# One output store per block of 32 tokens in place of four, in a one-core hybrid attention and PEER step

## The chip, the cores and the metric

The kernel runs on one core of a Trainium2 chip. The metric is the device time in microseconds (us) of one execution; the figure given for a kernel is the median of several runs.

## The reference, cut to what matters

One layer of a streaming encoder is computed for 512 prompt tokens and 32 sample tokens of width 1024: two attention mixers merged by gates, and then PEER, a retrieval over 16384 experts. For each token PEER picks 16 experts in each of 8 heads, 128 in all, takes a dot product with each expert's row of `u`, and sums the experts' rows of `v` with the weights that come of it. The change lies where the last sum leaves the chip:

```python
x = x + out
x = x + _peer(_rms(x, ln2_g), peer_wq, peer_subkeys, peer_u, peer_v)
# in _peer, for a block of tokens t and its chosen experts e with weights g:
a = jax.nn.gelu(jnp.einsum('td,thkd->thk', t, u[e]))
return jnp.einsum('thk,thkd->td', (g * a.astype(jnp.float32)).astype(t.dtype), v[e])
# y_prompt = x of the prompt without its 16 meta tokens, y_sample = x of the sample
```

## The kernel before, in words

Tokens stand in five tiles: the sample tile of 32 tokens comes first, then four prompt tiles of 128. The work behind the attention is cut into **17 blocks** of 32 tokens (`BLOCKS`): one for the sample, four for each prompt tile. A block has 32 **columns** (`SG`). A column is one gather: GpSimd's queue (POOL) fetches 128 rows of `peer_uv`, one for each of 32 tokens times 4 groups, each row 8 KB (an expert's `u` and `v` side by side), 1 MB in all, into one of nine buffers `rows` (`RING`). Partition 32a + t of a column belongs to token t and group a.

For each column:

- VectorE (DVE) takes the dot product of the `u` half with the token's row in `ps_h` (`dot`, L2580), and after every second column prepares the argument of the gelu (`arguments`, L2587 to L2590).
- ScalarE (ACT) makes of that a weight and a 128 x 32 matrix `diag` (`diagonals`, L2117 to L2126).
- TensorE (PE) multiplies `diag` with the `v` half and adds to `ps_v` in PSUM (`mix`, L1793): 16 matmuls, in four groups of 256 output columns. Group a's 32 partitions of `ps_v` hold columns 256a to 256a + 255 of the block's 32 tokens.
- The gather of column c waits until the mix of column c - 9 is done (`s_pv`), since it reuses that buffer.

When a block's 32 columns are mixed, ACT copies `ps_v` into `yo`, one of two buffers of 128 x 256 (`block_out`, L2134), and issues the stores on its own DMA queue. PE begins the next block with the residual (`residual`, L1784) once the copy is done. ACT's program is fixed: it calls `block_out(n)` and right after it `diagonals` for the first two columns of the next block. `block_out` waits for `s_out` of the same `yo` buffer, so for the stores of two blocks earlier. The last wait of the program, on the SyncE queue (SP), is for all stores (L1293).

Beside all that, while blocks are mixed, the attention of the next tile runs in slices between the columns (`front`, spread over a tile's 128 columns by `ticks_at`); its weights come as 512 KB loads on SP's queue into four buffers `wch`. Behind the last tile's attention (about 1421 us) only columns are left. So three queues feed the core's 16 DMA engines: POOL's with the gathers, SP's with the weights, ACT's with the stores.

The stores before, in `block_out`:

```python
t = tile(i)
for a in range(GROUPS):
    dst = io.y_prompt[P * t + GROUP * g:P * t + GROUP * (g + 1), :] if t < 4 else io.y_sample[:, :]
    act.dma_start(dst[:, QD * a:QD * (a + 1)], yo[GROUP * a:GROUP * (a + 1), n % 2, :]).then_inc(s_out[n % 2], 16)
```

Here `GROUPS` is 4, `GROUP` 32 and `QD` 256: each store takes 32 partitions, 1 KB from each, to 32 rows of the output that lie 4 KB apart.

Of the kernel before, what the change touches and what calls it, by code (L numbers as in the profile page):

```python
# [28 lines left out]
P = 128  # L29
# [658 lines left out]
GROUP = 32  # L688
GROUPS = P // GROUP
# [3 lines left out]
NB = len(BLOCKS)  # L693
# [6 lines left out]
QD = D // GROUPS  # L700
# [19 lines left out]
def first_block(i):  # L720

    return BLOCKS.index((i, 0))
# [182 lines left out]
def stream(nc, io, m, sem):  # L905
# [22 lines left out]
    tan, weight, diag, yo, rows = m.tan, m.weight, m.diag, m.yo, m.rows  # L928
# [53 lines left out]
    def tile(i):  # L982
        return ORDER[i]
# [92 lines left out]
    def slot_of(p, j):  # L1076
        return place[(p, j)] % WRING
# [5 lines left out]
    def uses_of(p, j):  # L1083

        n = place[(p, j)]
        return len(loads[n % WRING:n + 1:WRING])
# [22 lines left out]
    with psum("ps_h", [P, D]) as ps_h, psum("ps_v", [P, QD]) as ps_v, \  # L1109
# [102 lines left out]
        s_out = [sem(f"s_out{i}") for i in range(2)]  # L1212

        @block.sync
        def _(sp):
            def load(p, j, src, n=D):
                if place[(p, j)] >= WRING:
                    p0, j0 = loads[place[(p, j)] - WRING]
                    sp.wait_ge(s_wu[slot_of(p0, j0)], uses_of(p0, j0))
                sp.dma_start(wch[slot_of(p, j)][:, 0:n], src).then_inc(s_wl[slot_of(p, j)], 16)  # L1220

            def load_gate(p, n):
                j, a = divmod(n, 2)
                load(p, G_AT + n, io.w_gate[DC * a + j, :, :, :].rearrange("p c k -> p (c k)"))

            def load_x(i):
                t = tile(i)
                if i >= 2:
                    sp.wait_ge(s_xc, first_block(i - 1))
                if t < 4:  # L1230
                    sp.dma_start(xb[i % 2][:, :], io.x_prompt[P * t:P * (t + 1), :]).then_inc(s_x[i % 2], 16)
                else:
                    sp.dma_start(xb[i % 2][0:DEC, :], io.x_sample[:, :]).then_inc(s_x[i % 2], 16)

            for p, members in enumerate(PASSES):
                if p:
                    i, = members
                    t = tile(i)
                    sp.wait_ge(s_av, 2 * H * (i - 1))
                    if p == 1:  # L1240
                        sp.wait_ge(s_tile_out.sem, s_tile_out.upto(DC))
                        sp.wait_ge(s_used, 1)
                    sp.dma_start(tab, io.tabs[:, t, :]).then_inc(s_tab, 16)
                    for n in range(WRING):
                        load(p, J_AT + n, io.w_row[n, :, :])
                    load_x(i)
                    for n in range(WRING, 12):
                        load(p, J_AT + n, io.w_row[n, :, :])
                    rest = DC * (COLS - 3 * 512)
                    load(p, J_AT + 12, io.w_row[12, :, 0:rest], rest)  # L1250
                    for k in range(2):
                        load(p, U_AT + k, io.w_uq[:, k, :], H * AQK)
                    load(p, V_AT, io.w_ukv[:, :])
                    for n in range(WRING):
                        load_gate(p, n)
                    sp.wait_ge(s_norm, p)
                    for dst, c0, w in OUT_COLS:
                        sp.dma_start(io.new_p[dst][META + P * t:META + P * (t + 1), :], pr[:, c0:c0 + w]).then_inc(s_new, 16)
                else:
                    for n in range(2 * SOON, 2 * SOON + WRING):  # L1260
                        load_gate(p, n)
                    for i in members:
                        load_x(i)
                    sp.dma_start(spare, io.keyb[:, :].rearrange("(a p) k -> p a k", a=GROUPS)).then_inc(s_spare, 16)
                for n in range(WRING + (0 if p else 2 * SOON), 2 * DC):
                    load_gate(p, n)
                if p:
                    for j in range(DC):
                        load(p, Z_AT + j, io.w_o[j, :, :])
                    for k in range(DC):  # L1270
                        load(p, O_AT + k, io.w_out[k, :, :])
                    for n in range(PH):
                        load(p, Q_AT + n, io.peer_wq[ASKED[n], :, :, :].rearrange("p c k -> p (c k)"))
                    continue
                sp.wait_ge(s_fav, 4)
                for k in range(DC // 2):
                    sp.dma_start(out_w[k], io.w_out[k, :, :]).then_inc(s_out_a.sem, 16)
                for j in range(WRING):
                    load(p, Z_AT + j, io.w_o[j, :, :])
                sp.wait_ge(s_ave, 2)  # L1280
                for k in range(DC // 2, DC):
                    sp.dma_start(out_w[k], io.w_out[k, :, :]).then_inc(s_out_b.sem, 16)
                for j in range(WRING, DC):
                    load(p, Z_AT + j, io.w_o[j, :, :])
                sp.wait_ge(s_fo, 1)
                sp.wait_ge(s_ot, 2)
                for c in ASK_REST:
                    sp.dma_start(ask_w[c], io.ask_rows[c, :, :]).then_inc(s_ask_w.sem, 16)
                sp.dma_start(key0, io.keyb[:, :]).then_inc(s_key0, 16)
                for c in ASK_RING:  # L1290
                    load(p, Q_AT + c, io.ask_rows[c, :, :])
            for a in range(2):
                sp.wait_ge(s_out[a], 16 * GROUPS * ((NB + 1 - a) // 2))  # L1293
            sp.wait_ge(s_new, 16 * 5 * (NP - 1))

        @block.gpsimd
# [24 lines left out]
        def _(pe):  # L1321
# [105 lines left out]
            def turn(i, u):  # L1427
                a = tile_unit(i, u)
                q = queries(i)
                pe.wait_ge(s_prob, a + 1)  # L1430
                if a:
                    pe.wait_ge(s_ptc, a)
                if u % H == 0 and earlies(i, u):
                    pe.wait_ge(s_pmc, earlies(i, u))
                for j, (c, r, _) in enumerate(chunks(i)):
                    ins = nc.tensor.transpose(turned()[0:r, j, 0:q], prob[a % 2][0:q, c:c + r], ident[0:q, 0:q])
                ins.then_inc(s_pt, 1)
# [57 lines left out]
            def few_turn(n):  # L1495
                pe.wait_ge(s_fprob, n + 1)
                if n:
                    pe.wait_ge(s_fptc, n)
                else:
                    pe.wait_ge(s_fcopy, 1)  # L1500
                for j, (c, r, _) in enumerate(few_chunks):
                    ins = nc.tensor.transpose(few_turned()[0:r, j, :], few_prob[n % 2][:, c:c + r], ident[:, :])
                ins.then_inc(s_fpt, 1)
# [310 lines left out]
        def _(act):  # L1814
# [314 lines left out]
            def block_out(n):  # L2129
                i, g = BLOCKS[n]  # L2130
                act.wait_ge(s_pv, SG * (n + 1))
                if n >= 2:
                    act.wait_ge(s_out[n % 2], 16 * GROUPS * (n // 2))
                nc.scalar.copy(yo[:, n % 2, :], ps_v[:, :]).then_inc(s_yo, 1)  # L2134
                act.wait_ge(s_yo, n + 1)
                t = tile(i)
                for a in range(GROUPS):
                    dst = io.y_prompt[P * t + GROUP * g:P * t + GROUP * (g + 1), :] if t < 4 else io.y_sample[:, :]
                    act.dma_start(dst[:, QD * a:QD * (a + 1)], yo[GROUP * a:GROUP * (a + 1), n % 2, :]).then_inc(s_out[n % 2], 16)

            for _ in front(0):
                pass
            for b in range(NCOL + LAG):
                if b % SLOTS == 0 and b // SLOTS + 1 < NP:
                    ahead = front(b // SLOTS + 1)
                if b >= SG and b % SG == LAG - 1:
                    block_out(b // SG - 1)
                if 2 <= b <= NCOL and b % 2 == 0:
                    diagonals(b - 2)
                if b < NCOL:  # L2150
                    n = b // SG
                    for _ in range(ticks_at(b)):
                        next(ahead)
                    if n + 1 < NB and b % SG == 17:
                        softmax(n + 1)
# [600 lines left out]
```

## Time and profile before

| what | value |
|---|---|
| median of 3 runs | 1814.53 us (1811.41 to 1815.37) |
| the profiled execution's own time | 1823.78 us |
| its span in the profile | 1822.0 us |
| DVE, PE, ACT, POOL busy, share of the span | 72%, 69%, 32%, 29% |
| moved by DMA | 696.47 MB, mean 382 GB/s |
| of it the gathers on POOL's queue | 570.53 MB |
| chain that ended last | DMA 36%, PE 27%, DVE 23% |

The span is the profiled execution without its start and end outside the trace. Busy shares are means over the whole span. The page cuts the span into 40 slices of 45.6 us and gives for each the busy tenths of every engine and the mean share in which the 16 DMA engines were busy. The stages are: up to 336 us the weights' first part and the first attention tiles; 336 to 1421 us columns with attention between them; 1421 to 1818 us columns alone; then the last store.

### The profile page before, as it was taken

To read this page: it belongs to the slowest core of one execution; us is meant where nothing else is said; L and a number is where in the kernel's file an instruction comes from. 1 tells how busy PE (TensorE), PEld (TensorE's weight loads), DVE (VectorE), ACT (ScalarE), POOL (GpSimd) and SP (SyncE) were. 2 spreads that over 40 slices of the span, in tenths; PEclk is the share of its full clock that TensorE was granted. 3 is DMA by queue.
4 is the path that set the end of the run, shared out by engine and by line. 5 is a ranking of instruction groups with operands and counts; after the bars stand their busy time and mean duration, and the time that the engine had idled before them with its cause. 6 is when DMAs were issued, how large, how long until landed. Compare 5 with 4: busy or idle time off the path is not lost.

```text
span 1822.0 us, 26376 instructions
## 1 busy us (share of the span) xinstructions
PE 1255.3 (69%) x9056; PEld 701.2 (38%) x9056; DVE 1308.2 (72%) x3842; ACT 581.8 (32%) x1997; POOL 524.0 (29%) x569
## 2 busy tenths in 40 slices
PE   8999776778877576778887576778877443434343
PEld 4668442444544233444544233445535111111111
DVE  5662676898766577798766676998676768686754
ACT  2332133433323333333422333343423322222222
POOL 0100123333323322332332222332322433333332
PEclk9989889787888687877898697887999555555555
DMA  6237399999999999899999999999999999999997
GB/s 263 72 100 279 157 394 423 401 425 424 426 424 423 422 416 422 351 407 405 422 422 422 424 422 390 408 389 386 424 422 424 424 427 426 426 427 424 427 421 301
DMA packets 119380, 696.47 MB, mean 382 GB/s; under 512 B 17983, under 2 KB 21118, under 8 KB 49102
## 3 DMA queue, kind: packets, MB, share of 16 engines
q0 software_dynamic: 78848, 570.53, 75.1%
q1 hardware_dynamic: 36686, 121.83, 17.3%
q10 hardware_dynamic: 3712, 2.43, 0.4%
q8 instruction: 72, 1.18, 0.2%
q14 instruction: 62, 0.51, 0.1%
HBM read 691.65 MB, written 3.02 MB: 381 GB/s over the span
## 4 chain that ended last, share of the span: by engine, by line
DMA 36%; PE 27%; DVE 23%; issue 5%; ACT 4%; POOL 1%; ACTq 0%; DVEq 0%; POOLq 0%
DMA rows<-in_peer_uv,index 26%; DVE rows L2580 9%; PE ps_v L1793 6%; PE ps_f L1546 4%; DMA wch<-in_w_row 4%; PE ps_f L1561 2%; DMA wch<-in_w_out 2%; PE ps_h L1773 2%; PE ps_f L1340 2%; DMA wch<-in_w_uq 1%; PE ps_f L1424 1%; PE ps_f L1464 1%; PE ps_f L1640 1%; DVE score L2289 1%; DMA wch<-in_peer_wq 1%
## 5 line engine op out<-in xcount | busy, mean ns | idle before, releaser
L2580 DVE CUSTOM_DVE_ANT_0 rows<-rows,ps_h 128x1024 f32<-128x1024 f32 x544 | 656.6, 1220 | 286.1 <-DMA rows<-in_peer_uv,index 235.5
L1317 POOL DMA_INDIRECT rows<-in_peer_uv,index x544 | 514.1, 945 | 1197.7 <-PE ps_v L1793 1007.9
L1793 PE MATMUL ps_v<-rows,diag 128*32 128x256 f32 x4352 | 424.7, 508 | 425.0 <-ACT diag L2126 425.0
L1793 PEld LDWEIGHTS ps_v<-rows,diag 128*32 128x32 f32 x4352 | 126.1, 131 | 677.8 <-ACT diag L2126 568.4
L2117 ACT ACTIVATE tan<-arg 128x2 f32<-128x2 f32 x272 | 55.5, 204 | 787.8 <-DVE arg L2590 764.0
L2120 ACT ACTIVATE weight<-tan,lead 128x1 f32<-128x1 f32 x544 | 180.8, 379 | 9.1
L2126 ACT ACTIVATE diag<-sel,weight 128x32 f32<-128x32 f32 x544 | 140.7, 305 | 0.1
L1546 PEld LDWEIGHTS ps_f<-bufh,wch 128*128 128x128 f32 x768 | 114.1, 233 | 21.2 <-issue 19.0
L1546 PE MATMUL ps_f<-bufh,wch 128*128 128x128 f32 x768 | 120.3, 322 | 0.0
L1340 PE MATMUL ps_f<-wch,bufh 128*128 128x512 f32 (+1 forms) x192 | 81.7, 565 | 27.8 <-DMA wch<-in_w_row 26.8
L1569 PE MATMUL ps_f<-wch,bufb 128*128 128x512 f32 x96 | 49.8, 650 | 19.7 <-DMA wch<-in_w_out 17.6
L1340 PEld LDWEIGHTS ps_f<-wch,bufh 128*128 128x128 f32 x192 | 32.8, 202 | 71.3 <-issue 34.9
L1640 PE MATMUL ps_f<-bufh,wch 128*128 128x128 f32 x384 | 53.8, 298 | 6.4 <-DMA wch<-in_peer_wq 6.3
L1640 PEld LDWEIGHTS ps_f<-bufh,wch 128*128 128x128 f32 x384 | 49.1, 207 | 18.9 <-issue 9.8
L1561 PE MATMUL ps_f<-bufq,wch 128*128 128x128 f32 x384 | 54.3, 300 | 1.3 <-ACT bufq L1957 1.2
L1561 PEld LDWEIGHTS ps_f<-bufq,wch 128*128 128x128 f32 x384 | 49.5, 209 | 13.0 <-issue 10.4
L1773 PE MATMUL ps_h<-hrows,rep 32*128 32x512 f32 x68 | 49.3, 861 | 2.8 <-DVE dots L2580 2.8
L2589 DVE TENSOR_TENSOR lead<-dots,halfw 128x2 f32<-128x2 f32 x272 | 43.9, 161 | 9.4
L2580 DVE DVE_READ_ACCUMULATOR2_ANT dots<- 128x1 f32 x544 | 44.9, 82 | 0.0
L1424 PE MATMUL ps_f<-bik,bufb 64*128 64x144 f32 (+2 forms) x96 | 38.9, 492 | 7.5 <-ACT kt L1878 6.7
L2587 DVE SCALAR_TENSOR_TENSOR cube<-dots 128x2 f32<-128x2 f32 x272 | 42.8, 158 | 0.6
L2590 DVE SCALAR_TENSOR_TENSOR arg<-cube,dots 128x2 f32<-128x2 f32 x272 | 42.2, 155 | 0.0
(389 smaller groups left out, 1690.0 us busy)
## 6 DMA issues: line engine op xcount, KB each, us to landing
wch<-in_w_gate SPq DMA_DIRECT2D x60, 512.0 KB, 8.1
wch<-in_w_row SPq DMA_DIRECT2D x36, 512.0 KB, 12.3
wch<-in_w_o SPq DMA_DIRECT2D x32, 512.0 KB, 7.7
wch<-in_w_out SPq DMA_DIRECT2D x24, 512.0 KB, 11.2
wch<-in_peer_wq SPq DMA_DIRECT2D x24, 512.0 KB, 12.6
rows<-in_peer_uv,index POOLq DMA_INDIRECT x544, 13.6
w_tok<-in_w_tok SPq DMA_DIRECT2D x4, 1640.0 KB, 13.6
wch<-in_w_uq SPq DMA_DIRECT2D x6, 384.0 KB, 12.3
```

What stands on the lines that cost most here:

```text
L1317: pool.indirect_dma_start(rows[c % RING][:, :, :].rearrange("p a d -> p (a d)"), None, io.peer_uv[:, :], at).then_inc(s_uv[c % RING], 16)
L1340: ins = nc.tensor.matmul(ps_f[:, 2 + c % 2, 0:cols], buf_h[:, k, :], w[:, b, :], start=(k == 0), stop=(k == DC - 1))
L1424: ins = nc.tensor.matmul(ps_f[0:q, u % 2, 0:nk], left, right, start=True, stop=True)
L1546: ins = nc.tensor.matmul(gated(p)[:, a, :], w[:, k, :], h_of(p)[:, k, 0:n], start=(k == 0), stop=(k == DC - 1))
L1561: ins = nc.tensor.matmul(blended(p, j)[:, x, :], w[:, x, k, :], ot_of(p)[:, x, k, 0:n], start=(k == 0), stop=(k == 3))
L1640: ins = nc.tensor.matmul(ps_f[:, 2 + n % 2, 0:x], w[:, k, :], h_of(p)[:, k, 0:x], start=(k == 0), stop=(k == DC - 1))
L1773: ins = nc.tensor.matmul(ps_h[:, 512 * j:512 * (j + 1)], rep[here, :, :].rearrange("p a m -> p (a m)"), hrows[i % 2][here, 512 * j:512 * ( ...
L1793: ins = nc.tensor.matmul(ps_v[GROUP * a:GROUP * (a + 1), :], diag[:, c % DRING, :], rows[c % RING][:, 1, QD * a:QD * (a + 1)], start=False ...
L2117: nc.scalar.activation(tan[:, s:s + 2], arg[:, s:s + 2], ACT.Tanh, scale=TANH).then_inc(s_tan, 1)
L2120: nc.scalar.activation(weight[:, s + j:s + j + 1], tan[:, s + j:s + j + 1], ACT.Identity, scale=lead[:, s + j:s + j + 1], bias=lead[:, s + ...
L2126: nc.scalar.activation(diag[:, (c + j) % DRING, :], sel[:, :], ACT.Copy, scale=weight[:, s + j:s + j + 1]).then_inc(s_diag, 1)
L2580: v.tensor_tensor_reduce(out=u, in0=u, in1=ps_h[:, :], scale=1.0, scalar=0.0, op0=ALU.mult, op1=ALU.add, accum_out=dots[:, c % KEEP:c % KE ...
```

## The change

The four stores of a block become one. Its source is all 128 partitions of `yo`; its target is the same region of the output, written as group, token, column: 4 x 32 x 256. It counts 16 instead of 64 on `s_out`, and the two waits on `s_out` are adapted. Nothing else differs.

```diff
@@ -1290,7 +1290,7 @@
             for a in range(2):
-                sp.wait_ge(s_out[a], 16 * GROUPS * ((NB + 1 - a) // 2))
+                sp.wait_ge(s_out[a], 16 * ((NB + 1 - a) // 2))
             sp.wait_ge(s_new, 16 * 5 * (NP - 1))
@@ -2130,13 +2130,12 @@
                 if n >= 2:
-                    act.wait_ge(s_out[n % 2], 16 * GROUPS * (n // 2))
+                    act.wait_ge(s_out[n % 2], 16 * (n // 2))
                 nc.scalar.copy(yo[:, n % 2, :], ps_v[:, :]).then_inc(s_yo, 1)
                 act.wait_ge(s_yo, n + 1)
                 t = tile(i)
-                for a in range(GROUPS):
-                    dst = io.y_prompt[P * t + GROUP * g:P * t + GROUP * (g + 1), :] if t < 4 else io.y_sample[:, :]
-                    act.dma_start(dst[:, QD * a:QD * (a + 1)], yo[GROUP * a:GROUP * (a + 1), n % 2, :]).then_inc(s_out[n % 2], 16)
+                dst = io.y_prompt[P * t + GROUP * g:P * t + GROUP * (g + 1), :] if t < 4 else io.y_sample[:, :]
+                act.dma_start(dst.rearrange("t (a c) -> a t c", a=GROUPS), yo[:, n % 2, :]).then_inc(s_out[n % 2], 16)
```

On ACT, at the end of each of the 17 blocks, between the copy of the block's sum and the first weights of the next block, the program reads (- before, + now; a DMA row gives the target's shape):

```order
 L2126 ACTIVATE diag<-sel,weight 128x32 x2
 L2134 COPY yo<-ps_v 128x256
-L2139 DMA out_y_prompt<-yo 32x256 x4
+L2138 DMA out_y_prompt<-yo 4x32x256
 L2117 ACTIVATE tan<-arg 128x2
 L2120 ACTIVATE weight<-tan,lead 128x1 x2
```

Four issues have become one in the same place, the target's outermost size is now 4 where each store had 32 before, and no other instruction has moved.

## Rows read from the trace of the kernel before

**Rows 1.** The page's slices: DMA's busy tenths and GB/s, 40 slices of the span

```profile
DMA  6237399999999999899999999999999999999997
GB/s 263 72 100 279 157 394 423 401 425 424 426 424 423 422 416 422 351 407 405 422 422 422 424 422 390 408 389 386 424 422 424 424 427 426 426 427 424 427 421 301
```

**Rows 2.** Windows from block end to block end (columns in the first line), core 0

```profile
core 0: us, PE busy (x) PEld busy (x) DVE busy (x) ACT busy (x) POOL busy (x), PEclk, DMA share, GB/s
336.00:426.00 90.00, 71.74 (x506) 44.83 (x502) 81.08 (x250) 32.09 (x120) 31.63 (x33) 0.79 1.01 416
...
730.00:826.00 96.00, 72.00 (x503) 43.33 (x505) 79.82 (x231) 34.10 (x120) 29.46 (x32) 0.79 0.94 382
826.00:919.00 93.00, 78.72 (x568) 47.51 (x569) 74.00 (x218) 34.98 (x132) 30.63 (x33) 0.83 1.00 414
...
1025.00:1134.00 109.00, 68.12 (x400) 30.96 (x401) 80.14 (x235) 39.01 (x115) 31.22 (x34) 0.80 0.99 410
1134.00:1227.00 93.00, 72.96 (x546) 48.71 (x544) 87.34 (x241) 33.50 (x115) 30.21 (x32) 0.85 0.99 398
1227.00:1322.00 95.00, 81.13 (x604) 52.63 (x596) 75.57 (x217) 37.38 (x132) 29.95 (x32) 0.86 0.98 405
...
1502.00:1582.00 80.00, 34.95 (x272) 10.85 (x276) 59.49 (x178) 21.17 (x83) 30.24 (x33) 0.53 1.01 426
...
1742.00:1818.00 76.00, 31.38 (x264) 9.68 (x264) 41.85 (x108) 20.66 (x80) 22.77 (x25) 0.52 0.88 369
```

**Rows 3.** The chain that ended last, in order of time (start, us, what), 1592 to 1652 us

```profile
1592.24 14.30 DMA rows<-in_peer_uv,index
1611.96 15.16 DMA rows<-in_peer_uv,index
1632.54 14.10 DMA rows<-in_peer_uv,index
```

**Rows 4.** DMA view of 1581 to 1592 us, one block's four stores in it

```profile
DMA packets 812, 4.64 MB, mean 422 GB/s; under 512 B 135, under 2 KB 263, under 8 KB 263
q0 software_dynamic: 618, 4.48, 96.8%
q10 hardware_dynamic: 192, 0.13, 3.7%
```

**Rows 5.** The instructions of the store's line and their landing

```profile
L2139 ACTq DMA_DIRECT2D out_y_prompt<-yo x64: 321/442/1249, 426.9 to 1820.0; - x64
DMA to landing us min/median/max: 5.0/6.3/8.3
```

**Rows 6.** Timeline at a block's end, 729 to 733 us, and at the program's end

```profile
729.95 1.74 ACTq L2139 DMA_DIRECT2D out_y_prompt<-yo  x4
731.73 0.20 ACT L2117 ACTIVATE tan<-arg 128x2 f32<-128x2 f32 x1 [1.82 <-issue]
...
1818.30 0.37 ACT L2134 COPY yo<-ps_v 128x256 f32<-128x256 f32 x1 [1.84 <-PE ps_v L1793]
1818.70 1.74 ACTq L2139 DMA_DIRECT2D out_y_prompt<-yo  x4
```

**Rows 7.** Issues of other transfers: two loads on ACT's queue, one three-dimensional load on SP's

```profile
L303 ACTq DMA_DIRECT2D bik_c<-in_bk_t x1: 560/560/560, 0.7 to 0.7; - x1
L304 ACTq DMA_DIRECT2D bik_c<-in_ik_t x1: 611/611/611, 1.3 to 1.3; - x1
L1264 SPq DMA_DIRECT2D kt<-in_keyb x1: 482/482/482, 83.3 to 83.3; - x1
```

**Rows 8.** DMA view of 1816 to 1822 us, nothing but the last block's stores in it

```profile
DMA packets 192, 0.13 MB, mean 22 GB/s; under 512 B 64, under 2 KB 192, under 8 KB 192
q10 hardware_dynamic: 192, 0.13, 7.9%
```

**Rows 9.** The page's queues (q1 SP's, q10 ACT's): packets, MB, share of 16 engines

```profile
q1 hardware_dynamic: 36686, 121.83, 17.3%
q10 hardware_dynamic: 3712, 2.43, 0.4%
```

**Rows 10.** Window of 732 to 742 us, columns as in Rows 2

```profile
732.00:742.00 10.00, 6.89 (x32) 2.93 (x33) 4.44 (x14) 5.15 (x15) 1.88 (x2) 0.50 0.52 186
```

## The prediction, made before the changed kernel ran

> **What bounds the kernel now.** I began with the slices of the page [rows 1]: from the sixth slice to the last but one the DMA engines show 9 tenths or more in all but one, at up to 427 GB/s, whatever PE and DVE do. Then I asked for windows cut at the block ends [rows 2]. There are 16 of them from 336 to 1818 us. In 11 the DMA share is 1.00 to 1.02; four are below, 0.94, 0.99, 0.99 and 0.98; the last shows 0.88, only because its final 11 us have no gathers left, and I count it with the 11 as full: 12. The chain of waits says the same from the other side: behind 1421 us it is one gather after another, each 14 to 15 us in flight, and from one to the next about 20 us, in which 8 columns go by [rows 3]. So a column costs 80/32 = 2.5 us [rows 2], the time in which 16 engines move 1 MB. A gather spends its 14 us in line behind five others; nothing that an engine of the core does faster there is worth anything. What counts is **how long each of the 16 DMA engines works**, and since a gather is complete only when all of its 128 rows have landed, the busiest of the 16 sets the pace.
>
> The four stores of a block are small in this: 192 packets, 3.7% of 16 engines over 11 us, which is 6.5 us of engine time, or 0.4 us on each engine if all take the same share [rows 4]. That all do is shown by the count. 192 is 4 times 48, and 48 is the 32 rows of a store and 16 completions, one from each engine; where the last four stores are alone, 64 of the 192 are under 512 B and 128 are of 1 KB [rows 8]. Each engine writes two rows of every store.
>
> **The change, part by part.**
>
> *The issues on ACT.* Four issues take 1.74 us, and the next block's first weights stand behind them [rows 6]. One issue of the new form is not in the trace. From below it is bounded by 0.32, the shortest of the stores now [rows 5]; from above by 0.61, an issue on ACT's queue early in the program; a three-dimensional load on SP's queue took 0.48 [rows 7]. I take 0.6, as those two are ACT's own and nothing else shows ACT issuing anything but 32 rows in the steady part. So ACT gets 1.74 - 0.6 = 1.1 us back at each block end (1.4 at most). Who waited for it: tan, weight, diag, then the mix, then the gather that reuses the buffer. In a stretch with the DMA engines full that gather would only stand in line earlier: nothing. At 729.95 it is different. The engines are half idle just behind it (0.52 over 732 to 742 us [rows 10]), and ACT's 1.74 us lie on the way there. I count 1.1 us of gain once. At 1134 and 1227 the stretches are below 1.00 too, but the chain there runs through PE and DVE rather than ACT's issues, so nothing.
>
> *The rows among the DMA engines.* Now the source's outermost size is 128 and the target's is 4. The trace has no transfer whose two sides differ in that, so the price is bounded from both sides. If the 128 rows are still dealt to 16 engines, each has 8 rows and one completion, as now: 0. If the deal follows the target's outermost size, four engines carry all 128 rows, 32 each, and the other twelve none. I take the second. The nearest row is SP's packet count [rows 9]: by the code its 264 transfers have 32463 rows, and with 16 completions each that would be 36687 packets; there are 36686. One completion is missing, and one transfer, the load of `brow`, has 15 rows: it ran on 15 engines. So the number of engines comes from the size of a dimension, and is not always 16; here a size of 4 allows four.
>
> This is also what the Trainium skill says (DMA: Bandwidth & Descriptors, section Why a DMA increments its semaphore by 16 and not by 1): the number of engines is the largest up to 16 that divides the slowest dimension of both sides, which would be 4 here. The trace agrees with it for 15 rows and 32 rows, and shows nothing for 4 against 128. By that rule the sum is the one that follows; without it, the first rival's.
>
> The price: a block's data now costs 6.5 us of engine time [rows 4]. Were all of it the 128 rows, a row costs 0.051 us; were completions as dear as rows, 0.034. Four engines do 24 rows more than before, so 24 x 0.034 to 24 x 0.051 = **0.8 to 1.2 us more on each of the four**, for each block. I take 1.1, near the upper end because the 64 small packets carry almost nothing. The other twelve get 0.4 us less, which helps nobody.
>
> *How often that counts.* 16 stores are followed by gathers. Where the engines are full (12 stretches), the four engines fall behind by 1.1 us, the gathers complete 1.1 us later, and so does everything behind: 12 x 1.1 = 13.2 us. In the four stretches below 1.00 something else leads; 0.06 x 96 = 5.8 us idle in the first and 1 to 2 us in the others hide 1.1 us each: 0. The cover there is that idle time.
>
> *The wait for the old store.* A store lands after 5.0 to 8.3 us [rows 5]. With 33 packets on an engine, taken in turn with gather rows of 0.31 us (96.8% of 176 us over 547 rows, the 618 packets less the 71 completions [rows 4]), it will take 33 x (0.31 + 0.05) = 12 us and about one more to start. `yo` is needed again two blocks, 160 us, later: free.
>
> *The end.* Now the last issue ends at 1820.4 and the span at 1822.0 [rows 6, 8]. With one issue the work starts about 1.1 us sooner, but four engines need 32 x 0.05 = 1.6 us for it instead of some 0.2 for the last 32 rows: 0, within 0.3.
>
> **Sum:** -1.1 + 13.2 + 0 = **+12.1 us**. The profiled execution takes 1823.8 us, 9.3 above the median of the runs; its sum would be 1835.9, and on the median it makes 1814.5 + 12.1 = 1826.6 us. Its own range: at the least the five stores behind 1421 us, where only gathers are left, and five of the others at 0.8, less 3 for ACT: +5. At the most 16 at 1.2: +19. So 1819.5 to 1833.5.
>
> **The rivals.**
>
> *Sixteen engines share the new store (faster).* It decides if the deal follows the 128 rows of the source. For it: both sides have 128 rows of 1 KB in the same order, and every 128-row transfer of SP's is on 16 engines by the packet count. Against: the 15-row load, and a target that has to be walked by group first. Then the DMA work is as before less 48 completions, ACT's 1.1 us count at 730, and the end comes 1.1 us sooner: 1814.5 - 2.2 = 1812.3. If ACT's issues also count at the two other block ends where the chain of waits passes through them (1322 and 1502, both with full engines, so I doubt it), 1810.1. The same page of the Trainium skill has a rule that speaks for this change (section Bandwidth: transfers under 64 KB are dominated by their descriptors, so batch them). The trace doesn't bear it out as a gain in time here: the rows of 1 KB stay what they are, and all four stores cost 0.4 us an engine [rows 4]. By that rule the time would be this rival's.
>
> *Four engines, but the ring hides it.* Nine buffers, six gathers in flight: a lag of 1.1 us on a queue of 14 us might be made good. For it: in 336 to 1421 us the chain is half PE and DVE. Against: a full engine cannot make good anything, and the share is 1.01. Something like a third of the forecast less ACT's part would be left: +2.5, 1817.
>
> *Four engines, and the attention pays too.* SP's weight loads run over the same four engines; where PE waits for them, the lag adds to stretches that I called free, and a 1 KB write could cost an engine more when it comes 32 times in a row. 16 x 1.2 = +19, 1833.7, or a little more.
>
> **How the numbers follow.** Forecast 0.66; sixteen engines 0.14; hidden by the ring 0.11; the attention pays too 0.09. What a measurement can tell from no change is about 0.2%, 3.6 us. Slower by more than that: 0.66 + 0.09 + 0.01 of the ring's case = 0.76. Faster: a third of the first rival, 0.05. The same: 0.19. The predicted time is the forecast's, 1826.6. The range takes in the forecast's own and the ring's case and leaves out the first rival and the tail above: 1815 to 1834.
>
> **What the changed profile would show.** ACT's queue has 3712 packets now, of which 17 x 192 = 3264 are stores. On four engines it would have 448 + 17 x 132 = 2692, on sixteen 448 + 17 x 144 = 2896: this settles the first rival alone. The store would land after about 13 us on four engines, under 5 on sixteen. Its issue should be one of 0.3 to 0.6 us. The stretches behind 1421 us should be 81 us each instead of 80, with the mean DMA share a little lower, as twelve engines run out of work now and then. I am wrong if stretches with full engines keep their length although 2692 packets are counted (then the ring hides it), or if they grow by 2 us or more (then a row costs more than 0.05 us).

## The result and the profile after

| | before | after |
|---|---|---|
| median of 6 runs each | 1814.95 us (1811.41 to 1817.31) | 1824.97 us (1821.5 to 1828.6) |
| profiled execution | 1823.78 us, span 1822.0 | 1826.15 us, span 1824.3 |

The ratio is 1.0050 with a 95% interval of 1.0031 to 1.0070: slower by 9 us, 6 to 13. The medians differ by 10.0. The forecast was +12.1 us, with a range of +0.5 to +19.5. The two profiled executions differ by only 2.4 us, since each is a single run. The part before the columns took 2.8 us less in the one of after. So from here on I compare lengths within a trace, from block end to block end.

The page of the changed kernel: its DMA lines of the slices, and its queues (packets, MB, share of 16 engines).

```profile
DMA  6227499999999999999999999999999999999996
GB/s 263 77 95 289 170 401 423 399 425 424 425 424 422 411 394 421 378 411 408 424 422 422 423 420 377 425 378 418 422 422 424 426 421 416 421 418 411 420 417 284
...
q0 software_dynamic: 78848, 570.53, 75.4%
q1 hardware_dynamic: 36686, 121.83, 17.1%
q10 hardware_dynamic: 2692, 2.43, 0.4%
```

The bytes are those of before, but ACT's queue has **2692 packets** in place of 3712 [rows 9]. The text above named two numbers: 2896 for sixteen engines, 2692 for four. It is four to the packet: 448 + 17 x (128 + 4). And behind the attention (the seven slices ahead of the last) GB/s is 411 to 421 where it was 421 to 427 [rows 1].

The last block's store alone, DMA view of 1818 to 1826 us of the changed kernel: 132 packets, 4 of them completions, against 192 and 64 [rows 8].

```profile
DMA packets 132, 0.13 MB, mean 16 GB/s; under 512 B 4, under 2 KB 132, under 8 KB 132
q10 hardware_dynamic: 132, 0.13, 5.4%
```

Stretches behind the attention in the changed kernel, cut at its own block ends (us, busy times, TensorE's clock, DMA share, GB/s). Before, the three that answer to them took 79.7, 80.5 and 79.7 us by the same copies, at 426 GB/s in the one shown [rows 2].

```profile
1499.50:1580.30 80.80, 34.56 (x268) 10.71 (x268) 59.51 (x177) 21.18 (x83) 30.00 (x33) 0.52 1.01 418
1580.30:1661.90 81.60, 35.68 (x268) 10.91 (x268) 60.64 (x178) 21.21 (x83) 30.02 (x33) 0.50 1.01 416
1661.90:1742.50 80.60, 35.67 (x268) 10.89 (x268) 59.42 (x177) 21.09 (x83) 29.89 (x33) 0.50 1.01 417
```

The engines of the core do the same work as before. The stretch is longer by about 1 us, and the DMA engines move 2% fewer bytes per us at the same recorded share. What has changed is the time recorded for a packet. The gathers' line in the DMA view of 1510 to 1730 us, of the kernel before and of the changed one:

```profile
q0 software_dynamic: 12814, 93.30, 100.6%
...
q0 software_dynamic: 12532, 91.25, 100.1%
```

By share and count, the mean packet of a gather is recorded with 0.276 us before (100.6% of 16 x 220 us over 12814) and 0.281 after. No view tells one engine from another.

The store on ACT, timeline of the changed kernel at three block ends, at 730 us, 1743 us and the last; and under it the issues among the instructions of the tile `yo`, shortest, median and longest in ns:

```profile
730.81 0.55 ACTq L2138 DMA_DIRECT2D out_y_prompt<-yo  x1
731.41 0.20 ACT L2117 ACTIVATE tan<-arg 128x2 f32<-128x2 f32 x1 [0.63 <-ACT yo L2134]
...
1742.78 0.55 ACTq L2138 DMA_DIRECT2D out_y_prompt<-yo  x1
1744.45 0.20 ACT L2117 ACTIVATE tan<-arg 128x2 f32<-128x2 f32 x1 [1.70 <-DVE arg L2589]
...
1820.16 0.37 ACT L2134 COPY yo<-ps_v 128x256 f32<-128x256 f32 x1 [1.84 <-PE ps_v L1793]
```

```profile
L2138 ACTq DMA_DIRECT2D out_y_prompt<-yo x16: 550/552/582, 423.9 to 1820.6; - x16
```

One issue takes 0.55 us in place of 1.74 for four [rows 6]. So ACT does get 1.2 us back at each block end. At 1743 it spends them waiting: the next weights start 1.7 us behind the copy because DVE's argument isn't there yet. That is the gain of the change going where it is worth nothing. At 730 the weights do start earlier.

How long the store is under way is seen in two windows of 4 us of the changed kernel, 1592 to 1596 and 1596 to 1600; the store was issued at 1580.7.

```profile
q0 software_dynamic: 227, 1.69, 99.8%
q10 hardware_dynamic: 36, 0.03, 2.4%
...
q0 software_dynamic: 236, 1.70, 101.3%
```

Its last packets fall between 11 and 15 us after the issue, where four stores landed after 6.3 [rows 5].

### The profile page after: what moved, and what is told of

Same layout as the page of the kernel before. It is cut to its first block, busy times and chain, and to the rows that moved or that the text cites. A ratio compares the mean times of both kernels' runs of the same rounds, so it can differ in the third digit from the quotient of the medians.

```text
span 1824.3 us, 26325 instructions
## 1 busy us (share of the span) xinstructions
PE 1243.4 (68%) x9056; PEld 694.1 (38%) x9056; DVE 1308.0 (72%) x3842; ACT 581.4 (32%) x1997; POOL 523.6 (29%) x569
## 3 DMA queue, kind: packets, MB, share of 16 engines
q10 hardware_dynamic: 2692, 2.43, 0.4%
## 4 chain that ended last, share of the span: by engine, by line
DMA 40%; PE 24%; DVE 22%; issue 6%; ACT 3%; POOL 1%; ACTq 0%; DVEq 0%; SPq 0%; POOLq 0%
DMA rows<-in_peer_uv,index 31%; DVE rows L2579 9%; PE ps_v L1793 5%; DMA wch<-in_w_row 4%; PE ps_f L1546 4%; PE ps_f L1561 2%; DMA wch<-in_w_uq 2%; DMA wch<-in_w_out 2%; PE ps_f L1340 2%; PE ps_h L1773 2%; DVE score L2288 1%; PE ps_f L1424 1%; POOL rows L1317 1%; DVE best L2287 1%; PE ps_f L1464 1%
## 5 line engine op out<-in xcount | busy, mean ns | idle before, releaser
L1340 PE MATMUL ps_f<-wch,bufh 128*128 128x512 f32 (+1 forms) x192 | 80.3, 556 | 28.9 <-DMA wch<-in_w_row 28.0
```

What stands on the lines that cost most here:

```text
L1340: ins = nc.tensor.matmul(ps_f[:, 2 + c % 2, 0:cols], buf_h[:, k, :], w[:, b, :], start=(k == 0), stop=(k == DC - 1))
```

## Experiments

Theory: a store whose target has 4 as its outermost size runs on four of the 16 engines; they get 24 rows more than before, 1.1 us a block, and where the engines are full the program is late by just that. The rivals: the single long transfer itself is the cost; the lag hits the attention's weights; a slow landing costs in any case; and, on the other side, ACT's issues are worth time. The kernels named "deal" and "flat" leave out the order of the output: they store the same bytes, in another order.

In the table, "behind" is the time from the end of block 12 to that of block 17 in the profiled execution, five stores, no attention; it is the difference of two starts of the `yo` copy. "Last four" is the same from the end of block 13 on, and "more per store" is a quarter of its difference to the kernel before. "Whole" is the ratio to the kernel before, run beside it, with its 95% interval.

| kernel | packets of ACT's queue | engines | behind, us | last four, us | more per store | whole |
|---|---|---|---|---|---|---|
| before | 3712 | 16 | 397.6 | 316.7 | | 1 |
| after | 2692 | 4 | 401.5 | 320.8 | 1.0 | 1.0050 (1.0031 to 1.0070) |
| deal16 | 3712 | 16 | 398.0 | 316.6 | 0.0 | 1.0015 (0.9999 to 1.0032) |
| deal8 | 3168 | 8 | 397.9 | 318.0 | 0.3 | 1.0019 (1.0000 to 1.0037) |
| deal4 | 2896 | 4 | 403.3 | 321.5 | 1.2 | 1.0070 (1.0047 to 1.0093) |
| deal2 | 2760 | 2 | 410.3 | 326.8 | 2.5 | 1.0159 (1.0133 to 1.0186) |
| flat | 2896 | 16 | 397.4 | 316.6 | 0.0 | 0.9987 (0.9971 to 1.0002) |
| late | 3352 | 4, from block 12 | 403.8 | 321.2 | 1.1 | 1.0027 (1.0011 to 1.0044) |
| early | 3052 | 4, up to block 11 | 396.3 | 316.6 | 0.0 | 1.0018 (1.0005 to 1.0030) |
| behind | 3712 | 16 | 398.1 | 316.6 | 0.0 | 0.9996 (0.9984 to 1.0008) |

The two columns are not equally sharp. Five of the kernels load the engines behind the attention alike (before, deal16, flat, early, behind). In "behind" they lie between 396.3 and 398.1 us, in "last four" between 316.55 and 316.66. The spread sits in the first stretch after the attention, which takes 79.7 to 81.4 us in these five. So a price per store is read from the last four.

### The number of engines, with four issues throughout

The edit to the kernel before, with l = 16, 8, 4, 2:

```diff
-                    act.dma_start(dst[:, QD * a:QD * (a + 1)], yo[...]).then_inc(...)
+                    act.dma_start(dst[:, QD * a:QD * (a + 1)].rearrange("(h l) c -> l h c", l=4), yo[...]).then_inc(...)
```

> Four stores a block as before, but each target is written with 16 as its outermost size (the 32 tokens of a store land in another order within the store; the rest is computed as before). Theory (the target's outermost size sets how many DMA engines carry a store, and the time comes from the load of the busiest): 16 engines, 4 x 48 = 192 packets a block, 3712 on ACT's queue; no change but for slower issues, 4 x 0.55 = 2.2 us in place of 1.74, which count once: 0 to +1 us on 1815. Stretches behind the attention 79.7 to 80.5 us as before. Rival (any target in three dimensions costs the DMA engines more): slower by 8 us or more, like the single store.

> The same with 8 as the outermost size (tokens of a store in another order). Theory: 8 engines, 4 x (32 + 8) = 160 packets a block, 448 + 17 x 160 = 3168 on ACT's queue. 16 rows on each busy engine in place of 8: 8 x 0.046 less 4 completions already there, +0.37 us a block; 12 blocks with full engines give +4.4 us. Rival (four issues cannot cost what one store cost): 0.

> The same with 4 as the outermost size (tokens of a store in another order): four issues a block, as before the change, but the load of the four engines is the changed kernel's. Theory: 4 x (32 + 4) = 144 packets a block, 2896 on ACT's queue; 24 rows more on each of four engines, +1.1 us in each of the last full stretches (80.8 us), +12 in all, and ACT's longer issues add 0 to 1: 1827. Rival (the single long transfer, or its one issue, is what costs, and not the four engines): within 3 us of before.

> The same with 2 as the outermost size (tokens of a store in another order). Theory: two engines with 64 rows each, 56 more than before: 56 x 0.046 = +2.6 us a block, stretches of 82.5 us behind the attention, 12 x 2.6 = +31 us, up to +38 if the idle time of the other four stretches no longer hides it: 1846 to 1853. 4 x (32 + 2) = 136 packets a block, 2760 on ACT's queue. Rival (the ring of nine buffers hides a lag): less than twice what deal4 shows.

The packet counts came out as expected in all four: each store has l completions. So the number of engines is the target's outermost size here, while the source's is 32 throughout. The `yo` copies on which the two columns rest, ends of blocks 12, 13 and 17 in the timeline of deal4, then of deal2:

```profile
1422.72 0.37 ACT L2134 COPY yo<-ps_v 128x256 f32<-128x256 f32 x1 [3.82 <-PE ps_v L1793]
...
1504.51 0.37 ACT L2134 COPY yo<-ps_v 128x256 f32<-128x256 f32 x1 [4.81 <-PE ps_v L1793]
...
1826.00 0.37 ACT L2134 COPY yo<-ps_v 128x256 f32<-128x256 f32 x1 [1.74 <-PE ps_v L1793]
```

```profile
1428.03 0.37 ACT L2134 COPY yo<-ps_v 128x256 f32<-128x256 f32 x1 [2.67 <-PE ps_v L1793]
...
1511.60 0.37 ACT L2134 COPY yo<-ps_v 128x256 f32<-128x256 f32 x1 [4.85 <-PE ps_v L1793]
...
1838.35 0.37 ACT L2134 COPY yo<-ps_v 128x256 f32<-128x256 f32 x1 [1.84 <-PE ps_v L1793]
```

The ends of blocks 13 and 17 in deal16, then in deal8; under them the end of block 13 before and after the change (those of block 17 are at 1818.30 and 1820.16):

```profile
1491.09 0.37 ACT L2134 COPY yo<-ps_v 128x256 f32<-128x256 f32 x1 [4.83 <-PE ps_v L1793]
...
1807.71 0.37 ACT L2134 COPY yo<-ps_v 128x256 f32<-128x256 f32 x1 [1.84 <-PE ps_v L1793]
```

```profile
1501.61 0.37 ACT L2134 COPY yo<-ps_v 128x256 f32<-128x256 f32 x1 [4.83 <-PE ps_v L1793]
...
1819.59 0.37 ACT L2134 COPY yo<-ps_v 128x256 f32<-128x256 f32 x1 [1.84 <-PE ps_v L1793]
```

```profile
1501.64 0.37 ACT L2134 COPY yo<-ps_v 128x256 f32<-128x256 f32 x1 [4.81 <-PE ps_v L1793]
...
1499.39 0.37 ACT L2134 COPY yo<-ps_v 128x256 f32<-128x256 f32 x1 [4.83 <-PE ps_v L1793]
```

And a window of deal2 between two of its block ends:

```profile
1593.50:1675.50 82.00, 35.31 (x268) 10.88 (x268) 60.01 (x178) 21.16 (x82) 29.96 (x33) 0.52 1.00 412
```

Against deal16, over the last four stores, one with 8 rows more on the busiest engines (deal8) costs (317.98 - 316.62)/4 = 0.34 us, with 24 more (deal4) (321.49 - 316.62)/4 = 1.22, with 56 more (deal2) (326.75 - 316.62)/4 = 2.53: 0.043, 0.051 and 0.045 us a row. The price is near to proportional to the load of the busiest engine, and it is paid on eight engines too. The whole time says the same, less sharply: +12.7 us (8.5 to 16.9) for deal4, where 12 was expected, and +28.9 (24 to 34) for deal2, a little short of the 31 to 38 expected. deal4 has four issues as before the change and is as slow as the change or slower, so the single long transfer is not the cost. The ring's rival wanted deal2 at less than twice deal4; it is at 2.1 times in the last four stores and 2.3 times in the whole.

deal8 should have cost 0.37 us a store, 4.4 us in all. The last four stores show 0.34; in the whole it is +3.4 us (0 to 6.7), which agrees but can't be told from deal16 by itself.

One thing did not fit. deal16 is slower in the whole by 2.7 us (0 to 6), where 0 to 1 was expected. Its four issues take 2.45 us in place of 1.74 (0.61 each), but its last four stretches are those of before; where the rest comes from stays open, if it is there at all.

### One issue on sixteen engines

```diff
-                act.dma_start(dst.rearrange("t (a c) -> a t c", a=GROUPS), yo[:, n % 2, :]).then_inc(...)
+                act.dma_start(dst.rearrange("t (a c) -> (t a) c", a=GROUPS), yo[:, n % 2, :]).then_inc(...)
```

> One store a block with the source as in the changed kernel, but the target taken as 128 rows of 1 KB in a row (the groups' parts of a block's output come to stand in another order). Theory: its outermost size is 128 on both sides, so 16 engines: 448 + 17 x 144 = 2896 packets on ACT's queue, landing under 6 us, stretches behind the attention 80.2 us as before the change; ACT gains 1.2 us a block, which counts once, and the end comes 1.1 us sooner: -2 us, 1813. Rival (one issue in place of four is worth time at most block ends): -8 us or more. Rival (one 128 KB store is bad however it is dealt): +8 us like the changed kernel.

This is the changed kernel with the deal alone put back. DMA view of 1573 to 1584 us, one store in it, and its issue at 1573.62:

```profile
q0 software_dynamic: 621, 4.53, 97.7%
q10 hardware_dynamic: 144, 0.13, 3.4%
```

```profile
1573.62 0.34 ACTq L2138 DMA_DIRECT2D out_y_prompt<-yo  x1
```

144 packets are 128 rows and 16 completions. The stretches are as before the change, and the whole is 2.4 us faster (5.3 faster to 0.4 slower), with -2 expected. So the target's form makes the difference of 11 us between flat and the changed kernel (0.9987 against 1.0050). The shorter issue (0.34 us against 0.55) could make 17 x 0.21 = 3.6 us of it at most. flat also writes its rows one behind the other instead of 4 KB apart; that the number of engines counts by itself is shown by deal16 to deal2, which all write the same addresses. What one issue in place of four can bring is some 2 us, 5 at the outside. One thing came out otherwise: the store lands after 6.9 to 8.2 us, where under 6 was expected and the four stores took 5.0 to 8.3 [rows 5]. It costs nothing that the stretches show. With this layout of `yo` a target that is right and has 128 outermost cannot be written: partition 32a + t goes to address 1024t + 256a, which is no single step.

### Where along the program it costs

Both take the changed store for some blocks and the four stores for the rest.

```diff
+                if parts(n) == 1:      # late: n >= 11; early: n < 11
+                    act.dma_start(dst.rearrange("t (a c) -> a t c", a=GROUPS), yo[:, n % 2, :]).then_inc(s_out[n % 2], 16)
+                else:
+                    for a in range(GROUPS):
...
```

> The single store for blocks 12 to 17 alone, whose stores lie behind the last attention (about 1421 us) and at the end; four stores before. Theory: five stores behind which the engines are full, 5 x 1.08 = +5.4 us in the stretches there (80.9 to 81 us in place of 80.2), the rest unchanged: +5. Rival (what the change costs comes from the attention's weight loads running over the slow engines): 0 to +1.

> The single store for blocks 1 to 11 alone, among the attention; four stores in the blocks after. Theory by the forecast's count: 7 of these 11 stores lie in stretches with full engines, 7 x 1.08 = +7.6, less 1.1 for ACT at about 730 us: +6 us; late and early add up to the changed kernel's +10 within 2 us. Rival (the compute between hides the lag among the attention): 0 to +3. Rival (weight loads make it worse there): +10 or more.

Late costs 4.9 us (2 to 8), as expected from five stores at 1.1, and its last four stretches show it (1.1 us a store). Early costs 3.3 us (0.9 to 5.4), below the 6 of the theory and nearer to the rival in which the compute between hides the lag. Together they make 8.2, within the 2 us of the +10. By these middle values more than half of the loss comes from the last quarter of the program, with a third of the stores; the two intervals overlap, so the split itself is rough.

Part of what is missing in early may be a larger gain at 730 us. The stretch from 730 on took 96.0 us before, and 95.7 to 97.1 in the other six kernels with four issues there (the four deals, late, behind). With one issue it took 92.5 (after), 94.8 (early) and 92.7 (flat): 1.2 to 3.5 us less, where I had counted 1.1.

### The stores behind the next block's first weights

```diff
                 if b >= SG and b % SG == LAG - 1:
                     block_out(b // SG - 1)      # now the copy alone
                 if 2 <= b <= NCOL and b % 2 == 0:
                     diagonals(b - 2)
+                if b >= SG and b % SG == LAG - 1:
+                    stores(b // SG - 1)
```

> Four stores as before the change, but issued after the first weights of the next block and not ahead of them, so that nothing of the next block waits for the 1.74 us of issues. Theory (the issues cover themselves behind full engines, but for about 730 us): -1 to -2 us, not distinguishable from no change. Rival (ACT's issues cost at most block ends): 16 x 1.7 = up to -27 us, at least -5.

The four issues are taken out of `block_out` into a function `stores`. The kernel is 0.7 us faster, 2.9 faster to 1.5 slower: no difference. The rival that ACT's issues cost at most block ends wanted 5 at least. Its stretch from 730 us on is 96.0 as before, although the first weights no longer wait. The four issues still stand ahead of ACT's attention copies (`bufq`, `kt`, L1878), which follow there; that these are what waited is my reading and wasn't tried.

### Where the DMA engines are not full

Both fetch half the bytes in each gather and leave out the `v` half: the mix adds the products of the dot in its place. The first has the four stores, the second the changed one.

```diff
-                pool.indirect_dma_start(rows[c % RING][:, :, :].rearrange("p a d -> p (a d)"), None,
-                                        io.peer_uv[:, :], at).then_inc(s_uv[c % RING], 16)
+                pool.indirect_dma_start(rows[c % RING][:, 0, :], None,
+                                        io.peer_uv[:, :].rearrange("e (a d) -> (e a) d", a=2), at).then_inc(s_uv[c % RING], 16)
...
-                                           rows[c % RING][:, 1, QD * a:QD * (a + 1)], start=False, stop=(k == SG - 1))
+                                           rows[c % RING][:, 0, QD * a:QD * (a + 1)], start=False, stop=(k == SG - 1))
```

> The kernel before, but each gather fetches rows of 4 KB (half the bytes; other rows of the table, and the mix adds the dot's products in place of the v rows). It is the base for the next kernel: the DMA engines should be busy for 60 to 75% behind the attention in place of all the time, and a block there should take 50 to 62 us in place of 80, paced by DVE (1.22 us a column and 0.46 us of arguments in two).

> The changed kernel with the same half gathers. Theory (the lag of four engines costs only where the engines are full): behind the attention each block leaves over 10 us of idle time on every engine, so the single store costs nothing there and ACT's 1.2 us at each block end may count: from 12 us faster to 1 slower than the four stores with half gathers, although its 2692 packets still go to four engines. Rival (the slow landing itself, or a lag that each gather must wait out, costs in any case): 5 us slower or more, like the change.

A window of lean_four, two blocks long (columns as in the windows above):

```profile
1350.00:1480.00 130.00, 70.66 (x544) 21.77 (x544) 117.45 (x357) 42.33 (x164) 60.57 (x65) 0.53 0.79 261
```

A block takes 65 us, above the 50 to 62 I expected, and DVE is busy for 90% of it. The DMA share is 0.79, also above what I had said, but each engine has some 13 us to spare in a block. Here the single store is not slower: 1598.15 us against 1599.96, ratios to the kernel before of 0.8777 (0.8756 to 0.8798) and 0.8822 (0.8794 to 0.8850). The copies of blocks 12 and 17, of lean_four and then of lean_one:

```profile
1284.76 0.37 ACT L2134 COPY yo<-ps_v 128x256 f32<-128x256 f32 x1 [4.13 <-remote]
...
1593.36 0.37 ACT L2134 COPY yo<-ps_v 128x256 f32<-128x256 f32 x1 [1.95 <-PE ps_v L1793]
```

```profile
1289.63 0.37 ACT L2134 COPY yo<-ps_v 128x256 f32<-128x256 f32 x1 [4.10 <-PE ps_v L1793]
...
1592.98 0.37 ACT L2134 COPY yo<-ps_v 128x256 f32<-128x256 f32 x1 [1.95 <-PE ps_v L1793]
```

308.6 us against 303.4: the edit that costs about 1 us a store with full engines costs nothing here. By these five stores it saves 1.05 us each, by the last four (243.9 us against 241.6, from block ends at 1349.48 and 1351.35) 0.56, and in the whole 2 us by the medians and 8 by the ratios, whose intervals just touch. So a gain is likely, in the direction of the 1.2 us by which the issues are shorter, but its size is not shown. The concentration on four engines costs nothing where they have time. Nor is the landing itself the cost: by the program nothing waits for a store but the reuse of its buffer two blocks later and the end.

## Why the prediction was right, point by point

- **The bound.** Right. Behind the attention the stretches follow the load of the busiest DMA engines and nothing else: flat and behind change what ACT does and leave the last four at 316.6 us, as before.
- **Four engines.** Right to the packet (2692). The inference from the 15-row load held, and deal16 to deal2 show it at four sizes (3712, 3168, 2896 and 2760 packets). It agrees with what the Trainium skill says (DMA: Bandwidth & Descriptors, section Why a DMA increments its semaphore by 16 and not by 1).
- **1.1 us a store (0.8 to 1.2).** Right where the engines are full: over the last four stores 1.0 in after, 1.1 in late, 1.2 in deal4. The working let the 24 rows stand alone and passed over three completions that each of the four engines is spared; deal4, which keeps them, is dearer than after and late by no more than 0.2.
- **ACT's issue, 0.6.** 0.55. Its gain of 1.1, counted once, at 730 us, measured 1.2 to 3.5 there, in one profile of each of three kernels: too small.
- **12 of 16 stores count.** The term of the sum that was too large. I had 13.2 us for it, 5 stores behind the attention and 7 among it. The five held (late: +4.9). The other part, 7.7 less ACT's 1.1, so 6.6, came to 3.3 (0.9 to 5.4). I had let a DMA share of 1.00 or more stand for "this stretch is paid in full". The chain of waits of the kernel before says otherwise. In the window of 1502 to 1742 us the gathers make 71.6% of the chain, in that of 336 to 1421 us 19.7% and the two largest kinds of weight loads 7.7% more, although the share is 1.00 or more in seven of the eleven stretches there. A share near 1 says that the engines always have something to do, not that the last wait of the stretch ends on them. So a lag that is partly hidden by PE and DVE among the attention is my reading of what is missing. It is argued and not shown: the larger gain at 730 us can account for 0.1 to 2.4 of the 3.3 us, and no run separates the two.
- **The end, 0.** From the last copy to the end of the span it is 3.7 us before (1818.3 to 1822.0) and 4.1 after (1820.2 to 1824.3). 0.4 more, a little over the 0.3 I gave.
- **The rival with sixteen engines** (1812.3) fell by the packet count; as a kernel of its own, flat, it measured 0.9987, 2.4 us faster, where I had put it at -2.2. Its landing, put under 5 us, took 6.9 to 8.2. **The ring's rival** fell with deal2 as an account of the whole; what spoke for it, a chain among the attention that is half PE and DVE, may still be why those stores cost less. **The attention pays too** fell with early.
- **The landing**, forecast at 13 us, lies between 11 and 15.
- **The mean DMA share** should have gone down a little. It did not: 1.01 as before, with 416 to 418 GB/s in place of 426. What shrank is the bytes per recorded busy time. That the other twelve engines run out of work now and then is therefore inferred, and no view shows it.

## What to carry to other kernels

Before you merge several stores into one, look at the outermost size on both sides of the new transfer: with 4 there, 12 of the 16 DMA engines take no part, and saving issues doesn't make up for it when the engines are full. A count of packets per queue shows the deal at once: rows plus one completion for each engine used. Issues saved on an engine that waits for data anyway are worth nothing; once the DMA engines had time to spare, the same edit cost nothing and seemed to gain a little. And before you count a stretch as paid in full because the DMA share in it is 1, look at how much of the chain of waits the transfers make there.

## What the runs showed that I had not expected

- The form of the target changes the time of an issue on ACT: with the same source, 0.34 us for 128 rows in a row (flat) and 0.55 for 4 x 32 x 256; 0.61 to 0.67 for the deals, with three dimensions and 32 partitions. The first issue of the new form in a program took 1.13 us in after, early and lean_one, and 1.14 in late, here by the line of after:

```profile
L2138 ACTq DMA_DIRECT2D out_y_sample<-yo x1: 1131/1131/1131, 334.0 to 334.0; - x1
```

- The loss does not show in the DMA share: it stays at 1.01 while GB/s falls by 2%. Whoever looks at the share alone sees no change.
- Half of the concentration costs as well: eight engines in place of 16 made a store 0.34 us dearer, visible in the stretches and lost in the noise of the whole.
